# A two-layer decoder trunk: keys turned token-major by a transposing DMA in the second layer, with new block sizes and a planner with another model of the DMA queues

## The reference, cut to what matters

```
hn = rms_norm(h);  proj = hn @ w_in                    # 7696 columns
A: g_log = log_sigmoid(g_lr @ w_gk2 + b_gk) / 16       # g_lr: 16 columns of proj
   S_t = diag(exp(g_t)) S_{t-1} + k_t^T v_t;  o_t = q_t S_t    # 4 heads, keys 128, values 256
   A = (rms_norm(o) * silu(g_out)) @ w_br_a
B: (mean over windows 2/4/8/16 - token) -> per-group map w_pool_mix -> scale -> @ w_br_b
C: gelu(u) * (tril(W_s) gelu(v) + b) in chunks of 128 -> @ w_br_c
h = h + (sig(ga)*A + sig(gb)*B + sig(gc)*C) @ w_out
h = h + relu(rms_norm(h) @ w_ff1)^2 @ w_ff2
```

## Time and profile before

| | us |
|---|---|
| median of 3 runs | 2384.38 |
| runs | 2384.38, 2616.1, 2383.14 |
| the profiled execution, own time | 2381.28 |
| its span, slowest core (core 5) | 2380.2 |
| spans of the other cores | 2371.6 to 2379.2 |
| PE busy | 2323.0 (98%) |
| DVE busy | 1273.8 (54%) |
| ACT busy | 886.3 (37%) |

### The profile page before, as it was taken

How to read it: one execution, slowest core, us unless ns; L and a number is a source line. 1 busy time by engine, 2 the same in 40 slices (tenths; PEclk the granted TensorE clock), 3 DMA queues, 4 the chain that set the end, 5 groups by cost and what they waited for, 6 DMA issues and landing times.

```text
span 2380.2 us, 40912 instructions; the slowest of 8 cores (2371.6 to 2380.2 us)
## 1 busy us (share of the span) xinstructions
PE 2323.0 (98%) x13392; PEld 1236.5 (52%) x13392; DVE 1273.8 (54%) x2231; ACT 886.3 (37%) x1810; POOL 245.9 (10%) x266
## 2 busy tenths in 40 slices
PE   6899999999999999999999999999999999999998
PEld 4576555546445454545455555564554454545453
DVE  3787776444465444434567776744434644434355
ACT  3877753222233121212456678322222421211133
POOL 2123222000000000000012233200000000000000
PEclk9999999999999999999999999999999999999999
DMA  9554936154186040406492467451815642222112
GB/s 162 143 165 122 186 125 142 71 97 111 70 159 103 1 72 1 76 1 116 127 164 74 149 137 157 100 135 63 142 72 107 126 65 36 36 37 36 18 59 93
DMA packets 219415, 229.41 MB, mean 96 GB/s; under 512 B 54315, under 2 KB 203307, under 8 KB 216106
## 3 DMA queue, kind: packets, MB, share of 16 engines
q0 software_dynamic: 83584, 78.45, 23.8%
q1 hardware_dynamic: 135626, 148.35, 20.9%
HBM read 240.41 MB, written 55.05 MB: 124 GB/s over the span
## 4 chain that ended last, share of the span: by engine, by line
PE 91%; DVE 3%; issue 2%; ACT 2%; DMA 2%; POOL 0%; DVEq 0%; ACTq 0%; SPq 0%; POOLq 0%
PE ps L454 90%; DMA wring<-w_in 1%; PE ps L467 1%; DVE U L428 0%; DMA Sf<-sgla 0%; DVE Sf L428 0%; ACT rsg L417 0%; DVE tmp L428 0%; ACT L417 0%; ACT tmp L417 0%; DVE sqg L425 0%; DVE lv L815 0%; ACT Sb L417 0%; DVE pt L425 0%; ACT xj L417 0%
## 5 line engine op out<-in xcount | busy, mean ns | idle before, releaser
L454 PE MATMUL ps<-hn,wring 128*128 128x384 bf16 (+1 forms) x6400 | 1245.4, 347 | 7.8 <-DVE sgt L425 1.7
L454 PEld LDWEIGHTS ps<-hn,wring 128*128 128x128 bf16 x6400 | 621.6, 98 | 545.4 <-issue 13.4
L454 PE MATMUL ps<-wring,a 128*128 128x512 bf16 x2176 | 476.0, 379 | 0.2 <-DVE a L425 0.2
L417 ACT ACTIVATE rl<-ps 128x384 f32<-128x384 f32 (+1 forms) x320 | 169.9, 532 | 637.9 <-PE ps L454 522.2
L425 DVE TENSOR_TENSOR h<-h,ps 128x512 f32<-128x512 f32 x340 | 233.1, 687 | 277.1 <-PE ps L454 276.1
L454 PEld LDWEIGHTS ps<-wring,a 128*128 128x128 bf16 x2176 | 212.8, 98 | 255.1 <-issue 0.7
L425 DVE TENSOR_TENSOR a<-rl 128x384 bf16<-128x384 f32 (+1 forms) x320 | 194.9, 612 | 276.0 <-ACT rl L417 268.0
L417 ACT ACTIVATE sg<-ps 128x384 f32<-128x384 f32 (+1 forms) x240 | 127.9, 533 | 450.3 <-PE ps L454 322.3
L454 PE MATMUL ps<-wring,hn 128*128 128x256 bf16 (+1 forms) x1088 | 193.7, 330 | 12.2 <-DMA wring<-w_in 10.8
L425 DVE TENSOR_TENSOR tmp<-sg,ps 128x384 f32<-128x384 f32 (+1 forms) x160 | 97.3, 608 | 154.4 <-ACT sg L417 79.1
L454 PEld LDWEIGHTS ps<-wring,hn 128*128 128x128 bf16 x1088 | 105.2, 99 | 79.3 <-issue 15.3
(11 more groups left out here) (137 smaller groups left out, 1777.6 us busy)
## 6 DMA issues: line engine op xcount, KB each, us to landing
wring<-w_ff POOLq DMA_DIRECT2D x32, 1024.0 KB, 13.1
wring<-w_in POOLq DMA_DIRECT2D x28, 1024.0 KB, 16.1
Sf<-sgla SPq DMA_DIRECT2D x64, 256.0 KB, 3.7
gla_s<-Sf SPq DMA_DIRECT2D x64, 256.0 KB, 2.8
H4s<-H_d SPq DMA_DIRECT2D x12, 768.0 KB, 8.5
OBs<-OB_d SPq DMA_DIRECT2D x12, 768.0 KB, 5.0
h_d<-h SPq DMA_DIRECT2D x17, 512.0 KB, 2.7
h<-h_d SPq DMA_DIRECT2D x17, 512.0 KB, 9.9
```

Source lines behind the costliest of these rows:

```text
L417: op(ACT, lambda: nc.scalar.activation(out=now(out), in_=now(in_), func=func, **kw), reads, writes, occ, 125.0, SETS.get(func))
L454: inst = nc.tensor.matmul(now(m[0]), m[1], m[2], start=m[3], stop=m[4], **kw)
```

## The change

- **Keys.** In layer 1, `gla_scan` turns the keys of a tile by one transposing DMA of 128x512 bf16 on SP, straight from `kq` to `ktok`. Layer 0 keeps the TensorE transposes and the copy. For this `kq` is laid out by tile and then head, and has one dependence for the four heads of k and one for those of q.
- **Norms in `out_block`.** All 17 tiles are turned by transposing DMAs, in both layers.
- **Blocks.** 3, 4, 4, 3, 3 tiles in place of 3, 3, 3, 4, 4; the places of `mg` follow.
- **Start.** `v1` is loaded right behind `v0` and ahead of `wglr` and `wgk2`; `wglr` is loaded at full width, padded with zeros, and without the memset; the load of x tile 6 no longer waits for `g0`, and tile 7 is the first that does; `bsp` and `rep` wait for the normalised tile 5.
- **Fuse.** The four products of `wpm` and the branch weights move from ahead of the first gate block into its third and fourth column groups.
- **Planner.** The queues are played as two streams that share the bandwidth, at 300 and 265 bytes per ns, with 100 ns per DMA and 2000 ns to landing. A transposing DMA counts with its plain bytes, and occupies SP for 1250 ns.

```diff
-BLK = [(0, 3), (3, 3), (6, 3), (9, 4), (13, 4)]
+BLK = [(0, 3), (3, 4), (7, 4), (11, 3), (14, 3)]
...
-    w_glr = din("w_glr", [DEPTH, 128, KT, 16])
+    w_glr = din("w_glr", [DEPTH, 128, KT, 32])
...
-        dma_at = [4000.0] * 5
+        clock = 4000.0
+        coming = []
+        moving = {3: collections.deque(), 4: collections.deque()}
+        landing = []
...
+        def free_up(n, fin):
+            for m in n.succ:
+                j = m.idx
+                t = fin + 250.0 if n.E is not PE or m.E is not PE else fin - n.lat
+                if t > rdy[j]:
+                    rdy[j] = t
+                need[j] -= 1
+                if need[j] == 0:
+                    ready[num[id(m.E)]].append(m)
...
+            upto = best[1] if best is not None else 1e12
+            while clock < upto and (coming or moving[3] or moving[4]):
+                on = [q for q in (moving[3], moving[4]) if q]
+                to = min([upto] + [clock + q[0][1] * len(on) for q in on] + ([max(clock, coming[0][0])] if coming else []))
+                for q in on:
+                    q[0][1] -= (to - clock) / len(on)
+                    if q[0][1] < 1e-6:
+                        m = q.popleft()[0]
+                        landing.append((to + m.lat, m.idx))
+                        landing.sort()
+                clock = to
+                while coming and coming[0][0] <= clock:
+                    _, i, e, work = coming.pop(0)
+                    moving[e].append([nodes[i], work])
+                if landing and landing[0][0] < upto:
+                    upto = landing[0][0]
+            if landing and landing[0][0] <= upto:
+                at, i = landing.pop(0)
+                free_up(nodes[i], at)
+                continue
...
-                dma_at[e] = at0 + (both + work - both / 2 if work > both / 2 else work * 2)
-                fin = dma_at[e] + (3500.0 if e == 3 else 2500.0)
+                coming.append((s + occ, n.idx, e, n.byts / (300.0 if e == 3 else 265.0) + 100.0))
+                coming.sort()
...
-            if turn:
-                n *= 3
-            record(self.E, fn, reads, writes, 500.0 if self.E is SP else 900.0, 0.0, byts=n, after=after)
+            record(self.E, fn, reads, writes, 1250.0 if turn else 500.0 if self.E is SP else 900.0,
+                   2000.0, byts=n, after=after)
...
-    mkb = [24, 30, 36, 42, 50]
+    mkb = [24, 30, 38, 46, 52]
...
-    kq_t = [nc.alloc_sbuf_tensor_at(f"kq{i}", [128, 2, 4, 512], BF16, offset=kq_off[i]) for i in range(2)]
-    kqh = [[[B(kq_t[i], kq_off[i] + (w * 4 + h) * KB, kq_off[i] + (w * 4 + h + 1) * KB) for h in range(4)] for w in range(2)] for i in range(2)]
+    kq_t = [nc.alloc_sbuf_tensor_at(f"kq{i}", [128, 2, 4, 4, 128], BF16, offset=kq_off[i]) for i in range(2)]
+    kqh = [[B(kq_t[i], kq_off[i] + w * 4 * KB, kq_off[i] + (w + 1) * 4 * KB) for w in range(2)] for i in range(2)]
...
-        memset(wglr.t[:, :, :], 0.0, [wglr])
...
-        plq.dma(wglr.t[:, :, 0:16], w_glr[l], writes=[wglr])
+        plq.dma(wglr.t[:, :, :], w_glr[l], writes=[wglr])
...
-        spq.dma(bsp.t[:, :, :], b_sp[l:l + 1].broadcast_to([128, 4, 128]), writes=[bsp], after=[slots[6]])
+        spq.dma(bsp.t[:, :, :], b_sp[l:l + 1].broadcast_to([128, 4, 128]), writes=[bsp], after=[hnB[5]])
...
-        spq.dma(rep.t[:, :], rep_d[l], writes=[rep], after=[slots[6]])
+        spq.dma(rep.t[:, :], rep_d[l], writes=[rep], after=[hnB[5]])
...
+    def by_tile(v):
+        return v.rearrange("p (j t) -> p j t", t=128)
...
-            tt(kq_t[par][:, 1, h, 0:Tp], ps.t[:, po:T], n.t[:, po:T], ALU.mult, [ps, n], [kqh[par][1][h]])
+            tt(kq_t[par][:, 1, 0:npr, h, :], by_tile(ps.t[:, po:T]), by_tile(n.t[:, po:T]), ALU.mult, [ps, n], [kqh[par][1]])
...
-            stt(kq_t[par][:, 0, h, 0:Tp], ps.t[:, po:T], QSCALE, e.t[:, po:T], ALU.mult, ALU.mult, [ps, e], [kqh[par][0][h]])
+            stt(kq_t[par][:, 0, 0:npr, h, :], by_tile(ps.t[:, po:T]), QSCALE, by_tile(e.t[:, po:T]), ALU.mult, ALU.mult, [ps, e], [kqh[par][0]])
...
-        kB, qB = kqh[par][1], kqh[par][0]
+        kB, qB = [kqh[par][1]], [kqh[par][0]]
         for j in range(npr):
             sl = slice(j * 128, (j + 1) * 128)
+            k = ktok[j % 2]
+            if l > 0:
+                spq.dma(k.t[:, :].rearrange("p (h d) -> p h d", h=4), kq[:, 1, j, :, :].rearrange("p h d -> p (h d)"), reads=kB, writes=[k], turn=True)
+            else:
+                ps = psum(RECUR)
+                pv = ps.t.bitcast(BF16)
+                pe_transposes([(pv[:, h * 128:(h + 1) * 128], kq[:, 1, j, h, :]) for h in range(4)], ident_bf.t[:, :], kB + [ident_bf], [ps])
+                vcopy(k.t[:, :], pv[:, 0:512], [ps], [k])
             ps = psum(RECUR)
-            pv = ps.t.bitcast(BF16)
-            pe_transposes([(pv[:, h * 128:(h + 1) * 128], kq[:, 1, h, sl]) for h in range(4)], ident_bf.t[:, :], kB + [ident_bf], [ps])
-            k = ktok[j % 2]
-            vcopy(k.t[:, :], pv[:, 0:512], [ps], [k])
-            ps = psum(RECUR)
-            pe_group([(ps.t[:, h * 128:(h + 1) * 128], kq[:, 1, h, sl], kq[:, 0, h, sl], True, True) for h in range(4)], kB + qB, [ps])
+            pe_group([(ps.t[:, h * 128:(h + 1) * 128], kq[:, 1, j, h, :], kq[:, 0, j, h, :], True, True) for h in range(4)], kB + qB, [ps])
...
-        if b == 0:
-            for g in range(4):
-                ps = psum()
-                pe_group([(ps.t[:, :], wpm.t[:, g, :], bbc[1][:, g, :], True, True)], [wpm, bbc[0]], [ps])
-                act(bbc[1][:, g, :], ps.t[:, :], AF.Copy, [ps], [bbc[0]])
+
+        def fuse(g):
+            ps = psum()
+            pe_group([(ps.t[:, :], wpm.t[:, g, :], bbc[1][:, g, :], True, True)], [wpm, bbc[0]], [ps])
+            act(bbc[1][:, g, :], ps.t[:, :], AF.Copy, [ps], [bbc[0]])
+
         for pi, (gw, sw, vw, ktn, src, k0) in enumerate(((ga, ba[0], ba[1], KT, hs, 0), (gb, bbc[0], bbc[1], 4, os_, 0), (gc, bbc[0], bbc[2], 4, os_, 4))):
             for m4 in range(4):
                 m = hf * 4 + m4
+                if b == 0 and pi == 0 and m4 > 1:
+                    fuse(2 * m4 - 4)
+                    fuse(2 * m4 - 3)
...
-            norm_to_hn(t, hB[t].t[:, :], hH[t], hj, hx[t % 2], turn=b >= 2)
+            norm_to_hn(t, hB[t].t[:, :], hH[t], hj, hx[t % 2], turn=True)
...
-        if t == 6:
+        if t == 7:
             wget(0, "g1")
-        spq.dma(xt[t % 3].t[:, :], rows(x_p, x_s, t), writes=[xt[t % 3]], after=[slots[4]] if t > 5 else ())
+        spq.dma(xt[t % 3].t[:, :], rows(x_p, x_s, t), writes=[xt[t % 3]], after=[slots[4]] if t > 6 else ())
...
-            wget(0, "v0")
+            wget(0, "v1")
...
-    glr = np.ascontiguousarray(f(w_in)[:, :, C_GLR:C_GLR + 16].reshape(DEPTH, KT, 128, 16).transpose(0, 2, 1, 3))
+    glr = np.zeros((DEPTH, 128, KT, 32), np.float32)
+    glr[:, :, :, 0:16] = f(w_in)[:, :, C_GLR:C_GLR + 16].reshape(DEPTH, KT, 128, 16).transpose(0, 2, 1, 3)
```

More of the change, by code:

```diff
@@ L1 @@
+import collections
 import numpy as np
@@ L270, in lay_out @@
                 ready[num[id(n.E)]].append(n)
-        for _ in range(len(nodes)):
+        def free_up(n, fin):
[7 more added lines that the diff above has]
+                    ready[num[id(m.E)]].append(m)
+        while len(order) < len(nodes):
             while oldest < len(tiles_in_order) and id(tiles_in_order[oldest]) in opened:
@@ L336, in lay_out @@
             order.append(n)
[L337 to L344, removed]
+            if not n.byts:
+                free_up(n, fin)
         return max(free), order, kof
@@ L677, in fn @@
             release((slot_sem[k], 16 * slot_cnt[k]), rs, ws)
-        record(POOL, fn, (), [b] + (first[2 * k:2 * k + 2] if n in (NSLOT, NSLOT + 1) else []), 900.0 * len(todo), 0.0, byts=byts)
+        record(POOL, fn, (), [b] + (first[2 * k:2 * k + 2] if n in (NSLOT, NSLOT + 1) else []), 900.0 * len(todo), 2000.0, byts=byts)
         views[order[n][0]] = [b] + vs
@@ L927, in gla_scan @@
                         if not begin:
-                            mms.append((osl, Sb[h].t[:, hf * 128:(hf + 1) * 128], kq[:, 0, h, sl], False, True, True))
+                            mms.append((osl, Sb[h].t[:, hf * 128:(hf + 1) * 128], kq[:, 0, j, h, :], False, True, True))
                 pe_group(mms, [vj[par][j], a] + (Sb[2 * h2:2 * h2 + 2] + qB if t0 + j else []), [ps])
```

## The result

The changed kernel takes **2402.2 us** (median of 4, 2401.6 to 2405.1) against 2385.1 before: ratio 1.0081, 95% interval 1.0068 to 1.0095. It is slower, where a gain of 0.5% was forecast, and lies outside the range.

The account below looks back on a forecast made before the run. PE, busy 2323.0 of 2380.2 us, was taken as the bound. Terms -8.9 (transposes) -1 (DVE copies) +3.3 (late keys) -4 (start) -1 (blocks) gave -11.6 us, so 2372.8 us, rounded to 2373; range 2358 to 2392 us.

Parts of the forecast that it names:

- Transposes, 8.9 us: Layer 1 keys and norms of blocks 0 and 1: 160 PE transposes removed, 3.6 plus 5.3 us off a full path.
- Start and blocks, 4 + 1 us: Reordered first loads gain 4 us; new block sizes gain 1 us from PE idle time in 80 to 120 us.
- Turning DMAs in `out_block`. Cost 0.: Twelve more norm turns in `out_block`, hidden by about 35 us before `ff1` reads them; bound 3 us per layer.
- I keep 3 us either way: Whole kernel: allowance for the new order of the other instructions, which comes with the new blocks.
- Late keys, +3.3 us: Last block's three key turns after 1400 us, beside refilled ring slots: 1.1 us of PE waiting each.
- the rival at 2403 us: Keys come late: all three last-block turns fully exposed beside the refilled ring, up to 11.2 us each; chance 0.15.
- The forecast's price for a late load, 1.12 us: After 1400 us: PE idled 1.12 us for a 9.49 us load of `Sf`; basis for 1.1 us per late key turn.
- Blocks, in the whole kernel: Block sizes 3, 4, 4, 3, 3: 1 us of gain taken, bounds gain 5 and loss 4 us.
- The forecast's own sign: Wrong if PE's idle time grows, or its busy time falls by much more or less than 9 us plus the clock's 2.4.

Follow-up runs that it names:

- bn_rl: Kernel before with all norms of `out_block` turned by DMA and the `rl` buffers moved 4 KB further on: 2381.1 us, ratio 0.9985.
- b_start: Kernel before with the changes of the start alone (`v1` ahead, `wglr` at full width, `bsp` and `rep` later, x tile 6 sooner): 2388.4 us, ratio 1.0046.
- b_norms: Kernel before with the norms of all five blocks in `out_block` turned by DMA, under the old planner: 2388.6 us, ratio 1.0015.
- a_rl: Changed kernel with the four `rl` buffers 4 KB further on, so the first no longer shares space with the second `hx`: 2411.6 us, ratio 1.0112.
- hx3: Changed kernel with three `hx` buffers in place of two in `out_block`, all turns still on DMA: 2406.4 us, ratio 1.0112.
- a_oldplan: Changed kernel with the planner of before; keys, norms, blocks, start and fuse as changed: 2411.4 us, ratio 1.0108.
- a_x3: Changed kernel with the new planner counting a transposing DMA at three times its bytes again: 2397.6 us, ratio 1.0053.
- u_blocks: Changed kernel with the block sizes of before (3, 3, 3, 4, 4) and the old places of `mg`: 2423.7 us, ratio 1.0168.
- a_half: Changed kernel with every refill of a ring slot loading only half its rows, instruction order kept: 2367.8 and 2363.5 us, two executions.

## Why the prediction was wrong

- **Transposes, 8.9 us.** Right in kind: the groups with `hx` are gone, `kq` is at 64. On a path that has gaps, it can't be measured alone; bn_rl, which takes away 5.3 us of them and has no new gap, gained 3 to 4 us.
- **Start and blocks, 4 + 1 us.** About right in size for the first 120 us: 5.9 us of idle time went at the median core. But the step stopped there. In b_start, which gained 2.9 us there, the kernel was 5 us slower as a whole, with more idle time at 240 to 280 us, in waits for samples. Time gained ahead of a place that waits for a DMA can turn into a longer wait at it.
- **"Turning DMAs in `out_block`. Cost 0."** This step failed. I looked for the reader of `hn`, which indeed has 35 us of cover, and not for the other things that a turn holds while it reads: one of two `hx` buffers, behind which VectorE's residual additions queue, and the space of `rl`. The changed kernel idles 12.2 us there on core 1, and 3 to 12 us by core. b_norms and bn_rl show the second of these. The first is read from the waits (52.9 us of VectorE for `hx`, 14 times) and from a_rl (12.56 us of VectorE, then 6.67 of TensorE); hx3, which should have eased it, was no faster, so their shares are not settled. a_oldplan shows that the turns cost nothing there in another order.
- **"I keep 3 us either way" for the new order.** This failed most. The planner's numbers alone cost 33 us in the kernel before, and the changed kernel in other orders (a_x3, a_oldplan) took 2397.6 and 2411.4 us. The old numbers give no better order for it, so what failed is the bound of 3 us for any new order, and not only the new model. I had the row for it: turns landing after 15.5 us and a load after 9.49 us, against the planner's 2 us and a margin. I used them for the keys alone, and not for every other DMA that the planner orders.
- **Late keys, +3.3 us, and the rival at 2403 us.** The rival's number, 2403 us, came true by luck. Its place (beside the refill) was right, but not its carrier: 2.5 us of waits for keys in the changed kernel, and 2400.0 us without them. In the old order the keys alone do cost 10 us. The forecast's price for a late load, 1.12 us from one row, was that of a load with other work ordered ahead of it; the same kind of load costs up to 8.9 us where the order has none.
- **Blocks, in the whole kernel.** The new sizes were a help under the new planner (u_blocks is 21 us slower than the changed kernel at the median, 6 to 34 us by execution), which I had put at 1 us.
- **The forecast's own sign.** It was to be wrong if PE's idle time grew. It grew from 57.2 to 72.1 us between the two cores compared above. PE's busy time, which was to fall by 9 us and 2.4 more, rose by 2.6, at a mean granted clock that fell from 0.998 to 0.994.

What is shown: in the changed order, half the bytes of the refill are worth about 36 us (a_half), through DMAs of SP's queue that land sooner, where they are worth 5 us in the order before. What stays open is how much of that each of samples, keys and norm turns carries in the changed kernel, since removing one changes the order of all the rest, and single orders differ by 10 us and more. By the Trainium skill, DMA: Bandwidth & Descriptors, Rules for kernel authors, DMAs issued from SP, ACT and GpSimd all run on the same 16 engines and interleave; the trace agrees that they share: a 256 KB store on SP took 12.59 us beside the refill on POOL, against 3.8 at the median.

## What to carry to other kernels

When engine programs are laid out by a planner, a change of its costs is a change of the whole kernel: compare what it assumes for a DMA with the slowest landings in the trace, not with the median. Before an operation moves from an engine to a DMA, list all that the DMA holds until it lands, source buffers and overlapping space included, and who queues behind each. And when undoing single parts doesn't bring the time back, keep the order and take away the suspected load (here half the bytes), with the same edit on the kernel before as a control: these two runs showed what the edits before them could not, since each of those changed the order as well.

## What the runs showed of the hardware

DMAs on SP's queue landed three to seven times later beside weight loads on POOL's queue, at a DMA share of 1.07 to 1.24: turns after up to 20.2 us in place of 3.0, 256 KB stores after 12.59 in place of 3.8. The issue of a turn, which holds SP's queue, also took up to 9.41 us in place of 1.23 (turns of `fx`). With half the bytes in the refill the slowest norm turn came down from 15 to 19 us to 11 to 13, by core. Gaps on TensorE cost more than their length: around the one at 240 to 280 us (8.6 us idle) the granted clock was 0.91 over 40 us, from a stretch at 1.2 GHz, which is 0.09 x 40 = 3.6 us of work more as an estimate.
